# An expert layer's ranking: one head ranked while the scores are still copied, and the first round looked up in two pairs of heads

## The chip, the cores and the metric

The kernel runs on one core of a Trainium2 chip. The metric is the device time of one execution in microseconds (us). Three runs are shown for the kernel before; each kernel also has one execution recorded by the profiler, from which all durations here are taken. What matters of the core: TensorE multiplies (PE; PEld is its weight load), VectorE (DVE) and ScalarE (ACT) do the elementwise work, GpSimd (POOL) issues the indirect DMAs, and SyncE (SP) issues nearly all other loads, in the order in which they are written.

## The reference, cut to what matters

Two transformer blocks follow each other over 256 tokens of width 1024; the first is attention with a convolution, the second latent attention with gated linear attention. Each ends in the same kind of expert layer, with 8 heads, 128 keys per half and 16384 experts, of which each head of each token uses 16:

```
q = (h @ w_q).reshape(B, L, HEADS, 2, HALF)
s = einsum('blhpd,pnd->blhpn', q, sub_keys)               # 2 x 128 scores a head
top_s, top_i = top_k(s, 16)
cand_s = top_s[..., 0, :, None] + top_s[..., 1, None, :]  # 256 candidates
cand_i = top_i[..., 0, :, None] * NKEYS + top_i[..., 1, None, :]
best_s, best_pos = top_k(cand_s.reshape(..., 256), 16)
idx = take_along_axis(cand_i.reshape(..., 256), best_pos, axis=-1)
gate = softmax(best_s)
out = sum over heads and picks of (gate * gelu(u[idx] . h)) * v[idx]
```

## The kernel before, in words

**The expert layer is computed densely.** Instead of gathering rows, the kernel multiplies all 128 x 128 experts' `u` rows with all 256 tokens, applies gelu, multiplies each result by its gate (zero for an expert that a token did not pick), and multiplies with all `v` rows. Each of the two blocks (b = 1, 2) thus has these stages: `wq` (16 units of weights: the queries), scores, `u` (128 units), `v` (128 units). A unit is 512 KB, loaded by SP into a ring of four slots. Each unit is split into a high and a low part, in two halves of 128x512: ACT makes the high part (line 2320), DVE the low one (line 2323), and PE multiplies half by half (lines 935 to 937: three matmuls for each of a unit's eight 128-row parts, 24 a unit). The split parts have a ring of four halves (`HLRING`), so ACT and DVE can be at most four halves ahead of PE. ACT also applies gelu to each unit's result, two units behind (line 2358, `take_unit`).

**Scores and ranking.** PE computes the scores of two groups of 128 tokens, 16 score rows each (line 2276). ACT copies them to SBUF in eight pieces, each of two heads (`peer_act_scores`, line 2286). DVE waits for all eight (line 2793) and then ranks. The rank work of one head is nine slots (`topk_part`, lines 2368 to 2397: max, index and replace over both key halves, twice; 256 sums; the same over those). Four heads are a round; the four rounds are tokens 0 to 127 heads 0 to 3, heads 4 to 7, then the same for tokens 128 to 255. After the 36 slots of a round come 16 lookup slots (`lookup_part`, lines 2406 to 2449), which turn the picks into expert numbers and the best scores into gates: slot 0 converts and shifts the scores, slot 1 splits a position into its two ranks, slots 2 to 13 find the keys (12 operations of 512 elements: line 2424 compares, 2428 multiplies, 2430 sums), slots 14 and 15 normalise the gates and write the cells' numbers `picks_at`. A round has 52 slots (`ROUND_SLOTS`), all four 208.

**Where the slots go.** The u stage is written out for its first 111 units. DVE does one slot behind each half of a unit (`between(n)`, n the number of the half, line 2795), and a second one behind halves 7, 15, 23 and 31 (`LEAD`, `LEAD_EVERY`), so that it is four slots ahead from then on. The splits of halves 0 to 3 were made before the scores, so DVE starts with the slots and its first split is that of half 4. Between slot 14 and the gates, ACT's exp must have run: `peer_act` has it behind four fixed units (`exp_at`, line 2743). It changes ACT's function table, and the next gelu changes it back.

**The gates of tokens 0 to 127 go over DRAM.** Rounds 0 and 1 give 8 heads x 16 picks, which POOL scatters into `gates_dram[b]`, one indirect DMA of 128 cells for each of the 128 picks (`pool_scatter`, line 2477). Before the 16 DMAs of a head POOL waits until those of the head before have landed (they add to cells). Round i is released by `picks_ready` (line 2446). SP loads the gates back at the start of the v stage: `peer_loads` waits until all 128 scatters have landed (line 2903), loads the first four gate tiles (line 2885), and goes on with the v units (line 2911) and further gate tiles in turn. The four loads of v units 0 to 3 (line 2870) stand ahead of that wait. DVE multiplies activations by gates (line 2592), ACT and DVE split the product (lines 2648, 2654), and PE multiplies with v (lines 2243, 2244).

**The gates of tokens 128 to 255** are made by PE in the last 16 steps of the u stage from one-hot rows (line 2553); they need the end of round 3.

## Time and profile before

| | us |
|---|---|
| runs shown | 2224.8, 2226.89, 2227.07 |
| their median | 2226.89 |
| span of the profiled execution, first to last instruction | 2213.0 |
| time of the profiled execution around its span | not shown |
| PE busy | 2163.7 (98%) |
| DVE busy | 1691.2 (76%) |
| ACT busy | 1305.5 (59%) |
| POOL busy | 446.1 (20%) |
| mean granted clock of PE | 0.996 |

The span is the time from the first to the last instruction of one profiled execution; a run's time is that of the whole program. Busy shares are averages over stages. "Idle before" in a row is the time in which the row's engine did nothing ahead of it, and the arrow names what ended that time, as far as semaphores show it. The granted clock is the share of full speed that PE's clock had: 1.00 is 2.4 GHz and 0.50 is 1.2 GHz. All times of rows are us from the start of the span.

### The profile page before, as it was taken

What the parts mean: (1) busy time and instruction counts of PE and PEld (TensorE: products, weight loads), DVE (VectorE), ACT (ScalarE), POOL (GpSimd) and SP (SyncE); (2) the same over time, 40 slices, a digit from 0 to 9 for tenths busy, and PEclk for the clock granted to TensorE, in tenths of its full rate; (3) what the DMA queues carried; (4) which work ended last, traced back from release to release, by engine and by line L of the source; (5) the groups of instructions that cost most, each with busy time, mean ns of one, the idle gap of its engine ahead of it and who ended that gap; (6) DMA issues with size and microseconds to landing.
All of it is one profiled execution on the core that took longest, in us unless ns stands there. A gap on an engine that the chain in (4) does not pass through costs nothing.

```text
span 2213.0 us, 48254 instructions
## 1 busy us (share of the span) xinstructions
PE 2163.7 (98%) x15536; PEld 1992.3 (90%) x15536; DVE 1691.2 (76%) x3690; ACT 1305.5 (59%) x2727; POOL 446.1 (20%) x277
## 2 busy tenths in 40 slices
PE   8999999999999999999999999999999998999999
PEld 2888899999999888888889988999999997888887
DVE  4787769998889777777656866769988797777777
ACT  3577556556687555555555554656665695555554
POOL 0000000766674000000000000002666682000000
PEclk9999999999999999999999999999999999999999
DMA  8777545777755666666455434556777745666665
GB/s 329 262 238 246 176 148 188 200 194 191 198 136 134 217 214 213 212 214 214 151 162 176 149 108 151 198 162 191 198 192 195 190 112 149 214 213 214 213 213 169
DMA packets 191118, 422.88 MB, mean 191 GB/s; under 512 B 54288, under 2 KB 88336, under 8 KB 190624
## 3 DMA queue, kind: packets, MB, share of 16 engines
q1 hardware_dynamic: 150112, 413.73, 57.4%
q0 software_dynamic: 36864, 0.15, 4.5%
q10 hardware_dynamic: 4032, 7.64, 1.0%
q8 instruction: 56, 0.92, 0.2%
q14 instruction: 54, 0.44, 0.1%
HBM read 403.48 MB, written 17.96 MB: 190 GB/s over the span
## 4 chain that ended last, share of the span: by engine, by line
PE 92%; DVE 3%; ACT 2%; issue 1%; DMA 1%; POOL 0%; DVEq 0%; ACTq 0%; POOLq 0%
PE ps L2243 21%; PE ps L935 15%; PE ps L937 15%; PE ps L936 15%; PE ps L2244 11%; PE ps L960 5%; PE ps L2553 3%; PE ps L1866 1%; PE ps L1844 1%; DMA ring<-stream 1%; PE ps L2276 1%; PE ps L2166 1%; DVE ring_lo L614 1%; ACT arena L679 1%; PE ps L1858 1%
## 5 line engine op out<-in xcount | busy, mean ns | idle before, releaser
L2243 PE MATMUL ps<-csplit,hl 128*128 128x512 f32 x2048 | 711.9, 393 | 13.1 <-issue 12.0
L2477 POOL DMA_INDIRECT gates<-gbuf,picks_at x256 | 441.5, 1724 | 907.1 <-issue 482.9
L2244 PE MATMUL ps<-csplit,hl 128*128 128x256 f32 x2048 | 572.7, 280 | 0.0
L935 PE MATMUL ps<-hsplit,hl 128*128 128x256 f32 x2048 | 569.6, 278 | 0.0
L936 PE MATMUL ps<-hsplit,hl 128*128 128x256 f32 x2048 | 566.4, 277 | 0.0
L937 PE MATMUL ps<-hsplit,hl 128*128 128x256 f32 x2048 | 566.3, 277 | 0.0
L2320 ACT CAST hl<-ring 128x512 fp32r<-128x512 f32 x562 | 342.5, 620 | 263.7 <-PE ps L937 239.4
L2243 PEld LDWEIGHTS ps<-csplit,hl 128*128 128x128 f32 x2048 | 385.6, 188 | 98.9 <-issue 12.4
L2323 DVE TENSOR_TENSOR hl<-ring,hl 128x512 fp32r<-128x512 f32 x562 | 384.9, 690 | 87.7 <-ACT hl L2320 50.8
L2660 DVE TENSOR_TENSOR hl<-ring,hl 128x512 fp32r<-128x512 f32 x508 | 351.1, 692 | 68.7 <-ACT hl L2650 55.8
L2244 PEld LDWEIGHTS ps<-csplit,hl 128*128 128x128 f32 x2048 | 387.4, 189 | 0.0
L935 PEld LDWEIGHTS ps<-hsplit,hl 128*128 128x128 f32 x2048 | 384.9, 188 | 0.1
L936 PEld LDWEIGHTS ps<-hsplit,hl 128*128 128x128 f32 x2048 | 385.0, 188 | 0.0
L937 PEld LDWEIGHTS ps<-hsplit,hl 128*128 128x128 f32 x2048 | 384.5, 188 | 0.0
L2650 ACT CAST hl<-ring 128x512 fp32r<-128x512 f32 x508 | 314.4, 619 | 74.7 <-PE ps L2244 74.7
L2648 ACT CAST csplit<-arena 128x256 fp32r (+1 forms) x256 | 104.0, 406 | 243.9 <-DVE arena L2592 226.9
L2654 DVE TENSOR_TENSOR csplit<-arena,csplit 128x256 fp32r<-128x256 f32 x256 | 109.0, 426 | 123.0 <-ACT csplit L2648 123.0
L2358 ACT ACTIVATE arena<-ps 128x256 f32<-128x256 f32 (+1 forms) x272 | 103.1, 379 | 13.6 <-PE ps L937 12.2
L936 PE MATMUL ps<-n_hi,ring_lo 128*128 128x256 f32 (+1 forms) x352 | 99.7, 283 | 0.0
L2949 POOL MEMSET arena<- 128x1024 f32 x1 | 1.0, 951 | 422.9 <-PE ps L937 422.9
L2592 DVE TENSOR_TENSOR arena<-arena,gring 128x128 f32 (+1 forms) x256 | 72.6, 284 | 11.0 <-DMA gring<-gates 11.0
L686 DVE TENSOR_REDUCE arena<-arena 128x128 f32<-128x1024 f32 x32 | 62.3, 1950 | 17.6 <-ACT arena L679 17.6
(418 smaller groups left out, 3461.1 us busy)
## 6 DMA issues: line engine op xcount, KB each, us to landing
ring<-stream SPq DMA_DIRECT2D x675, 512.0 KB
s_area<-stream SPq DMA_DIRECT2D x48, 512.0 KB, 5.0
gates<-zeros SPq DMA_DIRECT2D x32, 512.0 KB, 5.1
gring<-gates SPq DMA_DIRECT2D x256, 64.0 KB, 4.1
gates<-gbuf,picks_at POOLq DMA_INDIRECT x256
arena<-xc ACTq DMA_DIRECT2D x2, 1024.0 KB, 15.5
arena<-keys ACTq DMA_DIRECT2D x2, 1024.0 KB, 6.7
gbuf<-consts ACTq DMA_DIRECT2D x1, 1120.0 KB, 5.1
```

The lines of the kernel that those rows point to most:

```text
L935: pe.matmul(out_ap, w[0], m[0], start=start, stop=False)
L936: pe.matmul(out_ap, w[1], m[0], start=False, stop=False)
L937: return pe.matmul(out_ap, w[0], m[1], start=False, stop=stop)
L960: mm = pe.matmul(ps[0:t.rows, t.bank, 0:t.cols], lhs, rhs, start=(t.start and i == 0), stop=(t.stop and i == last))
L2243: pe.matmul(ps[:, bank, :], w_hi, m_both, start=start, stop=False)
L2244: return pe.matmul(ps[:, bank, 0:T], w_lo, m_both[:, 0, :], start=False, stop=stop)
L2320: eng.copy(hl[:, hslot, 0, :], raw).then_inc(S("split_hi"), 1)
L2323: eng.tensor_tensor(hl[:, hslot, 1, :], raw, hl[:, hslot, 0, :].bitcast(F32), ALU.subtract)\
L2477: pool.indirect_dma_start(out=cells, out_offset=bass.IndirectOffsetOnAxis(ap=picks_at[:, i, c:c + 1], axis=0), in_=gates[:, i, c:c + 1], i ...
L2650: eng.copy(hl[:, hslot, 0, :], slot(unit)[:, part]).then_inc(S("split_hi"), 1)
L2654: ins = eng.tensor_tensor(csplit[:, cslot, 1, :], acts[:, c], csplit[:, cslot, 0, :].bitcast(F32), ALU.subtract)
L2660: eng.tensor_tensor(hl[:, hslot, 1, :], slot(unit)[:, part], hl[:, hslot, 0, :].bitcast(F32), ALU.subtract).then_inc(S("split_lo"), 1)
```

## The change

Three things are changed, all around the ranking, in both blocks.

- DVE waits for one of the eight score copies, not all, ranks the whole first head (nine slots), and only then waits for the other copies. From there `between(n)` does slot 9 + n behind each half n; the double slots are gone.
- Round 0 is cut in two pairs of heads. Each pair has 18 ranking slots and 8 lookup slots (`lookup_pair`): slot 0 does what slots 0 and 1 did, slots 1 to 6 are the 512-element operations, slot 7 does what slots 14 and 15 did. Each pair ends with its own `picks_ready`. Rounds 1 to 3 are as before.
- POOL waits for `picks_ready` before each head, for the first pair (heads 0, 1), the second (2, 3) or round 1. ACT's exp comes in five parts, the first two of 32 columns, behind units 6, 19, 41, 67 and 93.

```
-    LEAD, LEAD_EVERY = 4, 8
+    AHEAD = ITEM_SLOTS
+    PAIRS = 2
+    PAIR_SLOTS = ROUND_SLOTS // PAIRS
+    PARTS = PAIRS + ROUNDS - 1
...
+    def look_up(eng, x, c, step, out):
+        if step == 0:
+            rank = (rank1, rank2)[x][:, c].rearrange("p (r o) -> p r o", o=1).broadcast_to([P, 32, TOPK])
+            every = iota[:, 0:TOPK].rearrange("p (o a) -> p o a", o=1).broadcast_to([P, 32, TOPK])
+            eng.tensor_tensor(hit[:, c, :], rank, every, ALU.is_equal)
+        if step == 1:
+            keys = key_f[:, x, c].rearrange("p (h o a) -> p h o a", h=2, o=1).broadcast_to([P, 2, TOPK, TOPK])
+            h4 = hit[:, c, :].rearrange("p (h k) a -> p h k a", h=2)
+            eng.tensor_tensor(h4, h4, keys, ALU.mult)
+        if step == 2:
+            eng.tensor_reduce(out, hit[:, c, :], AX_X, ALU.add)
...
+    def lookup_pair(eng, b, pair, n):
+        c, heads = slice(pair * 32, pair * 32 + 32), slice(pair * 2, pair * 2 + 2)
+        best = picks_best[:, 0, :].rearrange("p (m k) -> p m k", k=TOPK)[:, heads, :]
+        g2 = gates[:, 0, :].rearrange("p (m k) -> p m k", k=TOPK)[:, heads, :]
+        if n == 0:
+            eng.tensor_copy(pos_f[:, c], picks_pos[:, c])
+            eng.tensor_copy(key_f[:, :, c], picks_key[:, :, c])
+            eng.tensor_tensor(g2, best, best[:, :, 0:1].broadcast_to([P, 2, TOPK]), ALU.subtract)\
+               .then_inc(S("gates_shifted"), 1)
+            eng.drain()
+            eng.tensor_scalar(rank1[:, c], pos_f[:, c], 1.0 / TOPK, -15.0 / 32, ALU.mult, ALU.add)
+            eng.drain()
+            eng.tensor_scalar(rank1[:, c], rank1[:, c], ROUND, ROUND, ALU.add, ALU.subtract)
+            eng.drain()
+            eng.scalar_tensor_tensor(rank2[:, c], rank1[:, c], -float(TOPK), pos_f[:, c], ALU.mult, ALU.add)
+        if 1 <= n < 7:
+            look_up(eng, (n - 1) // 3, c, (n - 1) % 3, chosen[:, (n - 1) // 3, c])
+        if n == 7:
+            eng.wait_ge(S("gates_exp"), PARTS * (b - 1) + pair + 1)
+            eng.tensor_reduce(gate_sum[:, 0, heads], g2, AX_X, ALU.add)
+            eng.scalar_tensor_tensor(chosen[:, 0, c], chosen[:, 1, c], float(P), chosen[:, 0, c], ALU.mult, ALU.add)
+            eng.drain()
+            eng.reciprocal(gate_sum[:, 1, heads], gate_sum[:, 0, heads])
+            eng.scalar_tensor_tensor(chosen[:, 0, c], chosen[:, 0, c], float(P), c_("token")[:, c], ALU.mult, ALU.add)
+            eng.drain()
+            z = gate_sum[:, 1, heads].rearrange("p (m o) -> p m o", o=1).broadcast_to([P, 2, TOPK])
+            eng.tensor_tensor(g2, g2, z, ALU.mult)
+            eng.tensor_copy(picks_at[:, 0, c], chosen[:, 0, c])
+            eng.drain().then_inc(S("picks_ready"), 1)
+        eng.drain()
...
+        ready = (PAIRS + 1) * (b - 1)
         for i in range(2):
-            pool.wait_ge(S("picks_ready"), 2 * (b - 1) + i + 1)
             for head in range(ITEMS):
+                pool.wait_ge(S("picks_ready"), ready + (1 + head // 2 if i == 0 else PAIRS + 1))
                 wait(pool, "scattered", 16 * sent)
...
-        exp_at = {(i * ROUND_SLOTS + ITEMS * ITEM_SLOTS - LEAD) // 2 + EXP_LAG: i for i in range(ROUNDS)}
+        shifted_at = [PAIR_SLOTS * pair + 2 * ITEM_SLOTS for pair in range(PAIRS)]
+        shifted_at += [ROUND_SLOTS * i + ITEMS * ITEM_SLOTS for i in range(1, ROUNDS)]
+        exp_at = {(n - AHEAD) // 2 + EXP_LAG: part for part, n in enumerate(shifted_at)}
...
-        dve.wait_ge(S("peer_s_copied"), 8 * b)
...
         def between(n):
-            done = n + min(n // LEAD_EVERY, LEAD)
-            ranking(done)
-            if n % LEAD_EVERY == LEAD_EVERY - 1 and n < LEAD * LEAD_EVERY:
-                ranking(done + 1)
+            ranking(AHEAD + n)
...
         def ranking(n):
             i, step = divmod(n, ROUND_SLOTS)
-            if i < ROUNDS and step < ITEMS * ITEM_SLOTS:
+            if i == 0:
+                pair, step = divmod(step, PAIR_SLOTS)
+                head, step = (2 * pair + step // ITEM_SLOTS, step % ITEM_SLOTS) if step < 2 * ITEM_SLOTS else (None, step)
+                if head is None:
+                    lookup_pair(dve, b, pair, step - 2 * ITEM_SLOTS)
+                else:
+                    topk_part(dve, 0, head, step)
+            elif i < ROUNDS and step < ITEMS * ITEM_SLOTS:
                 topk_part(dve, i, *divmod(step, ITEM_SLOTS))
...
+        dve.wait_ge(S("peer_s_copied"), 8 * (b - 1) + 1)
+        for n in range(AHEAD):
+            ranking(n)
+        dve.wait_ge(S("peer_s_copied"), 8 * b)
```

## Rows read from the trace of the kernel before

**Rows 1.** The page: span, and busy time of each engine (share of the span)

```profile
span 2213.0 us, 48254 instructions
...
PE 2163.7 (98%) x15536; PEld 1992.3 (90%) x15536; DVE 1691.2 (76%) x3690; ACT 1305.5 (59%) x2727; POOL 446.1 (20%) x277
```

**Rows 2.** Timeline, u to v in block 2: start, duration, engine, line, operation [idle before]

```profile
1842.11 0.28 PE L937 MATMUL ps<-hsplit,hl 128*128 128x256 f32 x1
...
1845.89 1.54 POOL L2477 DMA_INDIRECT gates<-gbuf,picks_at  x1 [1.90 <-issue]
...
1848.92 1.75 SPq L2885 DMA_DIRECT2D gring<-gates  x4
...
1852.19 0.76 PE L2243 MATMUL ps<-csplit,hl 128*128 128x512 f32 x1 [9.80 <-issue]
```

**Rows 3.** Waits of SP's queue: total us, times, longest

```profile
SPq L2885 <- DMA gates<-gbuf,picks_at: 9.0, 1, 9.0
```

**Rows 4.** Timeline, the same place in block 1

```profile
692.99 1.65 POOL L2477 DMA_INDIRECT gates<-gbuf,picks_at  x1 [0.30 <-issue]
...
700.91 1.86 SPq L2885 DMA_DIRECT2D gring<-gates  x4
...
703.10 0.28 PE L937 MATMUL ps<-hsplit,hl 128*128 128x256 f32 x1
...
705.63 0.76 PE L2243 MATMUL ps<-csplit,hl 128*128 128x512 f32 x1 [2.24 <-issue]
```

**Rows 5.** Timeline of POOL: the first scatter DMA of block 1 and of block 2

```profile
389.03 1.65 POOL L2477 DMA_INDIRECT gates<-gbuf,picks_at  x1 [387.58 <-DVEq L2446]
...
1528.38 1.56 POOL L2477 DMA_INDIRECT gates<-gbuf,picks_at  x1 [336.31 <-issue]
```

**Rows 6.** Timeline of ACT, block 1: the first of the eight score copies

```profile
317.84 0.69 ACT L2286 ACTIVATE s_area<-ps,small 128x512 f32<-128x512 f32 x1 [1.26 <-PE ps L2276]
```

**Rows 7.** Timeline of DVE, block 1: head 0, from its first slot to head 1

```profile
324.81 0.49 DVE L2370 MAX8 topbuf<-s_area 128x8 f32<-128x128 f32 x2 [7.51 <-ACT s_area L2286]
...
327.34 0.69 DVE L2323 TENSOR_TENSOR hl<-ring,hl 128x512 fp32r<-128x512 f32 x1
327.95 0.08 DVE L2382 MATCH_VALUE_LOAD picks_key<-topbuf,tmpbuf 128x8 f32 x1
...
333.47 0.69 DVE L2323 TENSOR_TENSOR hl<-ring,hl 128x512 fp32r<-128x512 f32 x1
```

**Rows 8.** PE in block 1: first u matmul (timeline), first gate matmuls (chain)

```profile
323.81 0.37 PE L935 MATMUL ps<-hsplit,hl 128*128 128x256 f32 x1
...
629.86 1.78 PE ps L2553 x16
```

**Rows 9.** Timeline of DVE, block 1: lookup slots of round 0 and splits

```profile
367.28 0.19 DVE L2407 CAST gbuf<-picks_pos 128x64 f32<-128x64 uint32 x1
...
369.27 0.69 DVE L2323 TENSOR_TENSOR hl<-ring,hl 128x512 fp32r<-128x512 f32 x1
...
370.64 0.69 DVE L2323 TENSOR_TENSOR hl<-ring,hl 128x512 fp32r<-128x512 f32 x1
...
386.28 0.21 DVE L2433 TENSOR_REDUCE gbuf<-gbuf 128x4 f32<-128x64 f32 x1
...
387.06 0.69 DVE L2323 TENSOR_TENSOR hl<-ring,hl 128x512 fp32r<-128x512 f32 x1
...
388.16 0.69 DVE L2323 TENSOR_TENSOR hl<-ring,hl 128x512 fp32r<-128x512 f32 x1 [0.17 <-issue]
```

**Rows 10.** Timeline of ACT, block 1: table load for the exp, and the one back

```profile
371.44 1.28 ACT L2749 ACT_TABLE_LOAD   x1
...
374.04 1.28 ACT L2358 ACT_TABLE_LOAD   x1
```

**Rows 11.** Stretches: us, busy (x) of PE, PEld, DVE, ACT, POOL, granted clock, DMA

```profile
705.60:708.70 3.10, 3.07 (x9) 2.67 (x10) 1.75 (x5) 0.80 (x3) 0.00 (x0) 0.50 0.34 100
...
1852.10:1855.50 3.40, 3.31 (x10) 2.86 (x11) 1.94 (x5) 1.37 (x4) 0.00 (x0) 0.50 0.60 187
```

More of the change, by code:

```diff
@@ L2420, in lookup_part @@
             c = slice(half * 32, half * 32 + 32)
-            if step == 0:
-                rank = (rank1, rank2)[x][:, c].rearrange("p (r o) -> p r o", o=1).broadcast_to([P, 32, TOPK])
-                every = iota[:, 0:TOPK].rearrange("p (o a) -> p o a", o=1).broadcast_to([P, 32, TOPK])
-                eng.tensor_tensor(hit[:, c, :], rank, every, ALU.is_equal)
-            if step == 1:
-                keys = key_f[:, x, c].rearrange("p (h o a) -> p h o a", h=2, o=1).broadcast_to([P, 2, TOPK, TOPK])
-                h4 = hit[:, c, :].rearrange("p (h k) a -> p h k a", h=2)
-                eng.tensor_tensor(h4, h4, keys, ALU.mult)
-            if step == 2:
-                eng.tensor_reduce(chosen[:, x, row][:, c], hit[:, c, :], AX_X, ALU.add)
+            look_up(eng, x, c, step, chosen[:, x, row][:, c])
         if n == 14:
-            eng.wait_ge(S("gates_exp"), ROUNDS * (b - 1) + i + 1)
+            eng.wait_ge(S("gates_exp"), PARTS * (b - 1) + PAIRS + i)
             eng.tensor_reduce(gate_sum[:, 0, :], g4, AX_X, ALU.add)
@@ L2746, in peer_act @@
             if s in exp_at:
-                i = exp_at[s]
-                act.wait_ge(S("gates_shifted"), ROUNDS * (b - 1) + i + 1)
-                act.activation(gates[:, i, :], gates[:, i, :], ACT.Exp).then_inc(S("gates_exp"), 1)
+                part = exp_at[s]
+                act.wait_ge(S("gates_shifted"), PARTS * (b - 1) + part + 1)
+                part_gates = gates[:, 0, part * 32:part * 32 + 32] if part < PAIRS else gates[:, part - PAIRS + 1, :]
+                act.activation(part_gates, part_gates, ACT.Exp).then_inc(S("gates_exp"), 1)
         first = groups_of(0)
```

## The prediction, made before the changed kernel was run

> **What bounds the kernel now.** I read the page's totals first: TensorE (PE) is busy for 98% of the 2213.0 us span [rows 1], so only a stretch in which PE stands still can be worth anything. The longest waits of PE put one such stretch at the start of the second block's v stage: PE ends its last u matmul at 1842.39 (1842.11 + 0.28) and starts its first v matmul at 1852.19, after 9.80 us idle [rows 2]. The "issue" behind that number names nothing, so I went to SP's own list of waits: SP stands 9.0 us at L2885, the load of the first gates, for the scatter's DMAs [rows 3]. In time the chain is: POOL issues the last scatter DMA at 1845.89, SP issues the gate loads at 1848.92, PE starts 3.27 us later [rows 2]. Hence **the scatter is late by 9.0 us in block 2, and PE pays for it**.
>
> Block 1 shows the same place without that wait. The last scatter DMA is issued at 692.99, about 8 us before SP comes to the gate loads at 700.91; PE is idle from 703.38 to 705.63, which is 2.24 us [rows 4]. This is the floor of the hand-over, set by SP's order (the gates go out behind the four v loads) and the path over DVE and ACT. In both blocks SP comes to the gate loads 2.47 us before the last u matmul ends (703.38 - 700.91; 1842.39 - (1848.92 - 9.0) = 2.47). So block 2 without the scatter's wait should look like block 1.
>
> **When the scatter runs.** In block 1 its 128 DMAs are issued from 389.03 to 694.64, 306 us or 2.39 us for each; in block 2 they start at 1528.38 and end at 1847.43 (1845.89 + 1.54), 319 us or 2.49 us for each [rows 2, 4, 5]. POOL has nothing before it; it waits for DVE's ranking.
>
> **The change, part by part.**
>
> *Scores copied while head 0 is ranked.* ACT makes eight copies of 0.69 us, the first from 317.84 to 318.53 [rows 6]; DVE has nothing to do for 7.51 us and starts ranking at 324.81 [rows 7]. The nine steps of head 0 cost, from 324.81 to 333.47 without the four splits between them (0.61 us each from 327.34 to 327.95), 8.66 - 2.44 = 6.22 us [rows 7]. Started at 318.53 they end at 324.75, just as the last copy ends. Cover: the copies. If it is gone, up to 6.22 us fall on DVE (rival 3). The head reads only the first copied bank, and a wait for one copy suffices.
>
> *Ranking ahead by nine slots, no double slots.* Before, DVE did 36 steps in the first 32 halves and was four ahead from then on; now it is nine ahead from the start and does one a half. DVE's work from half 4 to 32 thus falls by four steps, about 4 x 0.69 us. That matters, because DVE had no slack here: PE starts half h at about 323.81 + 1.36 h (323.81 for half 0, and 629.86 for the gate matmuls behind half 223, 224 halves later) [rows 8]; DVE begins split 47 at 387.06 and ends it at 387.75 [rows 9], and half 47 is due at 387.7 to 388.0. The old order was tight to a few tenths of a us.
>
> *Lookup in two pairs.* What a round of four heads did in 16 slots is now 2 x 8 slots. Six of each eight are the same 512-element instructions as before, 1.37 us with the split (369.27 to 370.64) [rows 9]. The other two hold what filled four slots. The first: full width it costs 369.27 - 367.28 - 0.61 = 1.38 us; the last: 388.16 - 386.28 - 0.61 = 1.27 us [rows 9]. A pair has half the columns, so each lies between one half (0.69 and 0.64) and the whole; for small instructions I take the whole, the nearest row. Then, by hand: split 9 starts at 334.1, split 10 at 334.1 + 0.61 + 1.38 = 336.1, split 16 six slots later at 344.3, the pair is ready at 344.3 + 0.61 + 1.27 = 346.2, and split 17 ends at 346.9. Half 17 is due at 323.81 + 17 x 1.36 = 346.9. So PE waits for 0 to 0.3 us there, and as much at half 43 with the second pair; I take 0 and keep 4 x 0.3 = 1.2 us for the range.
>
> A rule that speaks against this part: the Trainium skill ("VectorE: DVE Perf Modes", section on the TRN2 errata) says that an operation from SBUF pays a fixed cost per instruction beside its columns, so halving the width does not halve the time. By its formula, 32 fewer columns at 0.96 GHz save an estimated 0.03 us of each of 14 instructions, 0.2 us in a slot; the sum is the same with it, since split 17 is then in time by some tenths. With the halved prices it would be in time by over 1 us. No row here shows both widths of one instruction.
>
> *One more exp on ACT.* It costs ACT a table load of 1.28 us before it and one behind it; from the first to the second it also did the exp and the next two copies, 374.04 - 371.44 = 2.60 us [rows 10]. The new ones stand behind units 6 and 19. PE ends half 9 near 323.81 + 13.6 = 337.4; behind it ACT does copy 13 and a take (I take 1.1 us), and then these 2.60 us: copies 14 and 15 are there at 341.1, and DVE wants copy 14 at 344.3 - 2 x 1.37 = 341.6. Cost 0; it waits for `gates_shifted`, which DVE gives at half 9, before ACT gets there; queued behind it are ACT's copies for halves 14 and 15.
>
> *The scatter starts earlier.* Before, the first DMA came 0.87 us behind the end of DVE's last slot (388.16 to 389.03) [rows 5, 9]. Now it comes at 346.2 + 0.9 = 347.1, or 42 us earlier; in block 2 at about 1486.4. Its new waits: heads 2 and 3 need the second pair, ready at half 42 (about 382), and POOL gets to them after 32 DMAs, 347.1 + 32 x 2.49 = 427. Round 1 is ready five halves earlier than before, near 451, and POOL gets there at 347.1 + 64 x 2.49 = 506. Neither wait is felt. SP has nothing new in its order. In block 2 the scatter ends at 1486.4 + 319 = 1805, and SP comes to the gates at 1839.9. **It is early by 34 us**, so even 10% more per DMA costs nothing. In block 1 nothing is gained, since it was early already.
>
> *What is late next.* The path of block 1: from the gates' issue to the first v matmul 4.72 us (700.91 to 705.63) against 3.27 us in block 2 [rows 2, 4]. With 4.72 the start is 1839.92 + 4.72 = 1844.64 instead of 1852.19: 7.55 us gained. With 3.27 it is 9.0 us. I take 7.55, since then the loads meet the v loads, as in block 1. The clock: after either gap (2.24 and 9.80 us) the granted clock is 0.50, the 1.2 GHz level, for a little over 3 us [rows 11]; so that loss stays, and a gap as short as block 1's does not spare it.
>
> **Sum.** -7.55 (block 2's hand-over) + 0 (everything else) on a profiled span of 2213.0 us. The median of the shown runs is 2226.89, 13.9 us above the span; I take this as what lies around it, the same before and after. 2226.9 - 7.5 = 2219.4 us. A measurement here tells about 0.2%, 4.5 us, from no change.
>
> **Rivals.**
> 1. *The wait is not there in ordinary runs, or the scatter ends no earlier* (18%). The 9.0 us are one execution; a scatter 3% quicker than the profiled one has no wait to lose, and a POOL held up by something else (a full queue: it has pauses of 2 to 5 us now) would end as late as before. Against: 319 us of scatter with a 34 us margin, and 306 us in block 1. Time: 2226.9, or 2223 with half the wait.
> 2. *More than the floor* (7%). The gates land in 3.27 us, so PE is idle for 0.8 us only, and the clock stays high: 9.0 + about 1.5 us (five pairs of matmuls in 3.1 us that would take half as long). Time 2226.9 - 10.5 = 2216.4. Against: the clock row of block 1.
> 3. *The nine steps are not under the copies* (5%). Place: the start of each u stage. If DVE gets going only behind the last copy, or slows the copies, it is 6.22 us late with 1.26 us of slack at half 4 (due 329.3, split ends at 328.03): PE stands 5.0 us a block, and the restart at the low clock costs 1.5 more: 2 x 6.5 - 7.5 = +5.5, 2232.4 us. It decides once head 0 ends over 5 us behind the last copy (7.5 / 2 + 1.26). For it: DVE was without slack up to half 47. Against: the first bank is copied 6.3 us before the last.
>
> **The numbers.** The forecast has 70%, its own range being 2217.5 to 2221.5. The range must leave no more than 2 in 10 out: it reaches down to rival 2 and up to rival 1, 2216.5 to 2227.2. Faster by over 0.2%: the forecast, rival 2 and a small part of rival 1, 0.76; the same 0.19; slower 0.05.
>
> **What would show it.** POOL's first scatter DMA near 347 and 1486; its last in block 2 near 1804, before SP's gate loads; SP's wait at L2885 gone; PE's gap at the v stage of block 2 at 2.2 us instead of 9.8; the first MAX8 at 318.5, and PE without idle time around halves 17 and 43. Wrong if PE shows gaps in the u stage, if the first v matmul of block 2 still waits for the scatter, or if the gap shrinks in the profile and the runs do not follow.

## The result, and the profile after

| | before | after |
|---|---|---|
| median of the runs, us | 2225.24 (2219.74 to 2227.07, 5 runs) | 2211.13 (2208.31 to 2221.41, 5 runs) |
| ratio, 95% interval | | 0.9943 [0.9916, 0.9970] |
| span of the profiled execution, us | 2213.0 | 2219.6 |

The kernel became faster, by 14 us in the medians against 7.5 foretold, and 2211.13 lies below the range (2216.5 to 2227.2). Meanwhile the profiled execution of after is *longer* than that of before, by 6.6 us. Both need explaining, and the pace of PE, found below, has a part in both. The 14 us are also partly the luck of five runs each: over all groups below the mean gain is 9.1 us.

Here are the page's totals of after, then the timeline at the end of block 2's u stage (start, duration, engine, line, operation, [idle before]), which answers to [rows 2]:

```profile
span 2219.6 us, 48312 instructions
PE 2176.5 (98%) x15536; PEld 2003.8 (90%) x15536; DVE 1695.6 (76%) x3714; ACT 1310.8 (59%) x2733; POOL 433.1 (20%) x277
```

```profile
1796.20 1.54 POOL L2517 DMA_INDIRECT gates<-gbuf,picks_at  x1 [4.21 <-issue]
...
1855.69 1.86 SPq L2935 DMA_DIRECT2D gring<-gates  x4
...
1857.88 0.28 PE L937 MATMUL ps<-hsplit,hl 128*128 128x256 f32 x1
...
1860.45 0.47 PE L2243 MATMUL ps<-csplit,hl 128*128 128x512 f32 x1 [2.29 <-issue]
```

**The hand-over is as foretold.** The last scatter DMA goes out 59 us before SP comes to the gates, SP's list of waits no longer has the scatter in it, and PE is idle for 2.29 us instead of 9.80. From the first gate matmul to the first v matmul of block 2 it is 75.92 us instead of 83.43: 7.51 us gained, against 7.55 foretold. The starts of the scatter also come where they were put (POOL's timeline, block 1 and block 2):

```profile
350.36 1.65 POOL L2517 DMA_INDIRECT gates<-gbuf,picks_at  x1 [348.92 <-DVEq L2487]
...
1490.75 1.56 POOL L2517 DMA_INDIRECT gates<-gbuf,picks_at  x1 [294.46 <-issue]
```

Here the u stage began 3.61 us later (327.42 against 323.81), so 350.36 is 346.75 on before's time axis; 347.1 was forecast.

**The early head fits under the copies.** Timeline of block 1, head 0 and the first and last score copy:

```profile
321.45 0.69 ACT L2289 ACTIVATE s_area<-ps,small 128x512 f32<-128x512 f32 x1 [1.26 <-PE ps L2279]
322.17 0.49 DVE L2373 MAX8 topbuf<-s_area 128x8 f32<-128x128 f32 x2 [1.25 <-ACT s_area L2289]
...
327.71 0.69 ACT L2289 ACTIVATE s_area<-ps,small 128x512 f32<-128x512 f32 x1 [0.21 <-PE ps L2279]
...
328.43 0.49 DVE L2373 MAX8 topbuf<-s_area 128x8 f32<-128x128 f32 x2
```

Head 0 takes 322.17 to 328.43, 6.26 us (6.22 foretold), and head 1 starts just as the last copy ends.

**The pair's two crowded slots.** DVE's timeline, block 1: first and last instruction of slot 0, then of slot 7, each with the split behind it:

```profile
338.30 0.17 DVE L2464 CAST gbuf<-picks_pos 128x32 f32<-128x32 uint32 x1
...
339.28 0.19 DVE L2473 SCALAR_TENSOR_TENSOR gbuf<-gbuf 128x32 f32<-128x32 f32 x1
339.55 0.69 DVE L2326 TENSOR_TENSOR hl<-ring,hl 128x512 fp32r<-128x512 f32 x1
...
348.37 0.18 DVE L2478 TENSOR_REDUCE gbuf<-gbuf 128x2 f32<-128x32 f32 x1
...
349.16 0.17 DVE L2486 CAST picks_at<-gbuf 128x32 uint32<-128x32 f32 x1
349.50 0.69 DVE L2326 TENSOR_TENSOR hl<-ring,hl 128x512 fp32r<-128x512 f32 x1 [0.17 <-issue]
```

They cost 339.55 - 338.30 = 1.25 us and 349.50 - 348.37 = 1.13 us, where 1.38 and 1.27 were taken at full width: half the columns saved 0.13 and 0.14. The Trainium skill ("VectorE: DVE Perf Modes", section on the TRN2 errata) has a fixed cost per instruction, and this trace agrees: the same CAST takes 0.17 us at 32 columns and 0.19 at 64 [rows 9]. Split 17 starts at 349.50 and ends at 350.2; PE comes to that half at 327.42 + 17 x 1.36 = 350.5. So it is in time with 0.3 us to spare, and PE has no gap in either u stage of this execution.

**Where the 6.6 us went.** I cut both executions at PE's starts (us): scores to first gate matmul (u), first gate matmul to first v matmul (hand-over), and what lies between.

| profiled execution | time | start to scores | u, block 1 | hand-over 1 | v 1 to scores 2 | u, block 2 | hand-over 2 | rest |
|---|---|---|---|---|---|---|---|---|
| before | | 316.64 | 313.22 | 75.77 | 750.56 | 312.57 | 83.43 | 360.81 |
| after | 2221.41 | 320.26 | 313.04 | 75.69 | 751.84 | 323.70 | 75.92 | 359.15 |

Block 2's u stage is **11.1 us longer** in after, without a gap. The stretches of 50 us show how (us, busy and matmuls of PE, PEld, DVE, ACT and POOL, granted clock, DMA share, GB/s), after and then before:

```profile
400.00:450.00 50.00, 50.00 (x443) 50.00 (x443) 45.35 (x119) 30.43 (x58) 35.14 (x22) 1.00 0.76 197
550.00:600.00 50.00, 50.00 (x444) 50.00 (x443) 43.53 (x108) 30.31 (x59) 33.94 (x20) 1.00 0.77 191
1550.00:1600.00 50.00, 50.00 (x427) 50.00 (x427) 43.84 (x115) 29.61 (x57) 36.99 (x23) 1.00 0.74 187
1700.00:1750.00 50.00, 50.00 (x427) 50.00 (x426) 41.92 (x105) 29.78 (x57) 36.85 (x22) 1.00 0.76 188
```

```profile
400.00:450.00 50.00, 50.00 (x444) 50.00 (x443) 45.47 (x127) 30.56 (x59) 36.78 (x23) 1.00 0.79 191
...
1600.00:1650.00 50.00, 50.00 (x443) 50.00 (x443) 44.75 (x138) 28.17 (x56) 32.51 (x21) 1.00 0.77 194
```

PE is busy throughout, the granted clock is 1.00, and yet it does 427 matmuls in 50 us in one stage and 443 in the other: 1.41 us a half of a unit, or 1.36. I call these **the 1.41 pace and the 1.36 pace**. That makes the profiled executions of before and after incomparable in length, although each of their hand-overs can be compared.

### The profile page after: what moved, and what is told of

Its sections match the earlier page's. It is cut to its first block, busy times and chain, and to the rows that moved or that the text cites. A ratio compares the mean times of both kernels' runs of the same rounds, so it can differ in the third digit from the quotient of the medians.

```text
span 2219.6 us, 48312 instructions
## 1 busy us (share of the span) xinstructions
PE 2176.5 (98%) x15536; PEld 2003.8 (90%) x15536; DVE 1695.6 (76%) x3714; ACT 1310.8 (59%) x2733; POOL 433.1 (20%) x277
## 4 chain that ended last, share of the span: by engine, by line
PE 91%; DVE 3%; ACT 2%; DMA 1%; issue 1%; POOL 0%; DVEq 0%; SPq 0%; ACTq 0%; POOLq 0%
PE ps L2243 21%; PE ps L935 15%; PE ps L937 15%; PE ps L936 15%; PE ps L2244 11%; PE ps L960 5%; PE ps L2593 3%; DMA ring<-stream 1%; PE ps L1866 1%; PE ps L1844 1%; PE ps L2279 1%; PE ps L2166 1%; DVE ring_lo L614 1%; ACT arena L679 1%; PE ps L1858 1%
## 5 line engine op out<-in xcount | busy, mean ns | idle before, releaser
L2517 POOL DMA_INDIRECT gates<-gbuf,picks_at x256 | 428.5, 1674 | 832.6 <-issue 447.3
L2361 ACT ACTIVATE arena<-ps 128x256 f32<-128x256 f32 (+1 forms) x272 | 103.1, 379 | 13.4 <-PE ps L937 12.1
```

The lines of the kernel that those rows point to most:

```text
L2517: pool.indirect_dma_start(out=cells, out_offset=bass.IndirectOffsetOnAxis(ap=picks_at[:, i, c:c + 1], axis=0), in_=gates[:, i, c:c + 1], i ...
```

## The experiments

Each kernel is one edit of before or of after. Ratios are to before, run on the same chip in the same group; its median there stands with the first run of each group.

### The two kernels again, and the two halves of the change

First group; before 2225.27 (35 runs). `before_again` and `after_again` are unedited. `front_only` is before with the early head and without the double slots, its round 0 in one piece:

```
-    LEAD, LEAD_EVERY = 4, 8
+    AHEAD = ITEM_SLOTS
...
-            done = n + min(n // LEAD_EVERY, LEAD)
-            ranking(done)
-            if n % LEAD_EVERY == LEAD_EVERY - 1 and n < LEAD * LEAD_EVERY:
-                ranking(done + 1)
+            ranking(AHEAD + n)
...
+        dve.wait_ge(S("peer_s_copied"), 8 * (b - 1) + 1)
+        for n in range(AHEAD):
+            ranking(n)
```

`pairs_only` is after with no early head and with the double slots of before back in place.

> The kernel before, unchanged, as a control, with a new profile. Three theories for a gain of 12.7 us where 7.55 was forecast. T1: the change is worth the hand-over of block 2 alone (7.5 us); the rest is the pace of PE in a u stage, which has two levels in the two profiles (444 and 427 matmuls in 50 us, 11 us over a stage) and falls by chance. T2: in ordinary executions the scatter of the kernel before ends later than in its profile, and the wait at the gates is 12 to 20 us. T3: the order of DVE's and ACT's slots at the start of the u stage sets PE's pace, so that the change itself moves it. Time: T1, T2 and T3 all 2225 us, ratio 1.000. Profile: T1 a hand-over of block 2 of 8 to 11 us, and either pace; T2 a hand-over of 12 to 20 us at the fast pace; T3 a hand-over near 10 us and the slow pace in at least one u stage.

> The changed kernel, unchanged, as a control, with a new profile. Hand-over of block 2 near 1.6 us under all three. T1: ratio 0.9966 on enough runs, any pace. T2: ratio 0.992 to 0.994. T3: ratio 0.992 to 0.994, and the fast pace in both u stages more often than in the kernel before.

> Only the first part: head 0 ranked during the copies, nine slots ahead, no double slots; round 0 is looked up whole. The scatter starts near 382 instead of 389, and ends some 7 us earlier than before. T1: the wait of block 2 shrinks from 9.0 to about 2 us, the hand-over to about 3 us, gain about 7 us, ratio 0.997. T2: gain 7 us only, with 5 to 12 us of wait left, ratio 0.997. T3: the whole gain of 12.7 us or near it, ratio 0.9943, because the double slots are gone.

> Only the second part: round 0 in two pairs, scatter started by the first pair (near 356, 33 us earlier than before), with the wait for all eight copies and the double slots as before. DVE has no slack here: the first slot of a pair's lookup is 1.3 us, on top of double slots, so PE may stand for up to 1 us around halves 21 and 47 in each block. T1: gain 7.5 us less up to 2, ratio 0.997. T2: the whole gain, 0.994. T3: no gain from the pace, as the double slots stay: 0.997.

| | median (range, runs) | ratio, 95% interval |
|---|---|---|
| before_again | 2228.20 (2218.73 to 2232.62, 12) | 1.0021 [0.9996, 1.0046] |
| after_again | 2209.65 (2206.38 to 2220.03, 12) | 0.9936 [0.9916, 0.9957] |
| front_only | 2212.52 (2203.66 to 2230.04, 12) | 0.9947 [0.9921, 0.9973] |
| pairs_only | 2229.51 (2219.87 to 2239.20, 12) | 1.0023 [1.0001, 1.0046] |

Before's second profile has the 1.41 pace in both blocks (us, PE busy, granted clock, DMA share, GB/s), and its list of SP's waits has no scatter wait:

```profile
400.00:450.00 50.00, 50.00 (x427) 1.00 0.73 184
...
1550.00:1600.00 50.00, 50.00 (x427) 1.00 0.74 188
```

A u stage at the 1.41 pace gives the scatter 11 us more, so the 9.0 us wait of [rows 3] is not there. **Pairs alone**, which release the scatter in time for block 2 just as the whole change does, are 20 us slower than the changed kernel. Their PE stands at halves 17 and 24, where the double slots now meet the crowded slots of a pair, for 0.2 to 0.8 us each, and both u stages go over to the 1.41 pace: block 1 at half 17, block 2 at half 22, two halves ahead of the longer of its stops. A reading formed: the stops are small, but PE's pace after them costs up to 11 us a block.

**The first part alone has the whole gain.** front_only, whose round 0 is not cut in pairs, comes out at a ratio of 0.9947, where T3 had 0.9943 and T1 and T2 had 0.997 (0.9973 is the end of the interval, so they are not quite excluded). Its mean lies 10.4 us under before (4.9 to 15.5) and 3.4 us over after_again, with an interval from 1.7 us under to 8.8 us over. Its scatter starts only some 7 us earlier in the u stage than before's. So the part of the change that was made for the scatter, the pairs, wins nothing measurable on top of the part that gives DVE more room.

### Stalls placed by hand

Second group; before 2226.72 (31 runs). All three are after with four more operations of 0.69 us on DVE in each block, at different halves:

```
+            for _ in range({20: 4}.get(n, 0)):
+                dve.tensor_tensor(hit[:, 0:32, :], hit[:, 0:32, :], hit[:, 0:32, :], ALU.max)
+                dve.drain()
```

`stall_late` has `{180: 4}`, `work_spread` one each behind halves 64, 72, 124 and 180. `lead0` is before with `LEAD, LEAD_EVERY = 0, 8`: no double slots, so its scatter starts later and DVE has less to do early.

> The changed kernel with four more DVE operations (128x512, 0.76 us each with their drain) behind half 20 of both u stages, where DVE has about 0.9 us of slack: PE stands for about 2.1 us there. The first runs showed that PE holds one pace per burst, 1.36 or 1.41 us a half, and that a kernel with short stalls (pairs only) went from the first to the second behind its stall. T3, now: every stall, however short, draws the pace of the rest of the stage anew, mostly the slow one. Then each block loses 2.1 us and 0.053 us for each of 201 halves, 12.8 us: 25 us over the changed kernel, 2235 us, and the profile shows 1.36 before and 1.41 behind the stall. T1, where the pace falls by chance at the start of a stage alone: only the stalls, 4 us, 2214 us, and one pace on both sides of the stall.

> The same four operations behind half 180 in both blocks, where DVE has about 1.5 us of slack: PE stands for about 1.5 us. T3: the slow pace holds for the 41 halves left only, 2 x (1.5 + 2.2) = 7 us, 2217 us. T1: 3 us, 2213 us. The difference to the stall behind half 20 is 18 us under T3 and 1 us under T1.

> The same four operations, one each behind halves 64, 72, 124 and 180, where the slack of 1.5 to 2.2 us covers one: no stall. T3 and T1: the time of the changed kernel, 2210 us, ratio to the kernel before 0.993. If more DVE work alone costs time, it is over 2213 us.

> The kernel before without its four double slots (LEAD 0, not 4): DVE's slack at halves 16 to 47 rises from 0.0-0.4 to over 1 us, and the scatter is released four halves, 5.5 us, later. Where PE is fast in block 2, the wait at the gates must grow from 9.0 to about 14.5 us; where it is slow, the stage is 11 us longer and the wait about 3 us. T3: the stalls of the tight halves are gone, so the fast pace holds more often, and the two effects nearly meet: 2220 us, that is below the kernel before (2225) although its scatter is later. T1: the same mix of paces as before and a later scatter, 2228 us.

| | median (range, runs) | ratio, 95% interval |
|---|---|---|
| stall_early | 2223.64 (2218.52 to 2231.14, 10) | 0.9998 [0.9974, 1.0021] |
| stall_late | 2220.67 (2212.63 to 2234.74, 10) | 0.9999 [0.9970, 1.0028] |
| work_spread | 2214.39 (2207.77 to 2222.16, 10) | 0.9956 [0.9930, 0.9981] |
| lead0 | 2228.63 (2220.62 to 2233.25, 10) | 1.0015 [0.9990, 1.0039] |

The work as such is nearly free: work_spread has a ratio of 0.9956, near that of the changed kernel, though its 2214.39 is over the 2213 us set for it (this group has no run of after). The same work as one stall is not free: 9 us between the medians of work_spread and stall_early. But the 2235 us expected of stall_early was a miss, and so was its profile. PE stands for 2.1 us in each block and then goes on at the **1.36** pace (PE's timeline, then stretches as above, the last one right behind the stall):

```profile
357.81 0.36 PE L935 MATMUL ps<-hsplit,hl 128*128 128x256 f32 x1 [2.08 <-DVE hl L2326]
...
1501.82 0.36 PE L935 MATMUL ps<-hsplit,hl 128*128 128x256 f32 x1 [2.10 <-DVE hl L2326]
```

```profile
400.00:450.00 50.00, 50.00 (x444) 1.00 0.75 193
1550.00:1600.00 50.00, 50.00 (x444) 1.00 0.73 193
...
1501.80:1506.00 4.20, 4.18 (x22) 0.59 0.73 151
```

The stalls need no change of pace to cost 9 us: in this profile the halves up to 212 take 3.95 us more in block 1 and 4.25 us more in block 2 than the same halves of a stage of after at 1.36. Of that some 2.2 us are the standing, and most of the rest is the low granted clock behind it, 0.59 in the stretch shown, with matmuls every 0.213 us for a time.

"A stall costs the pace" is thus refuted as a rule; stall_late's block 1 did fall to the 1.41 pace behind its short stalls at halves 181 to 183, and its median of 2220.67 is above both forecasts (2217 and 2213). lead0 was a miss for T3 too, which had 2220; its 2228.63 is what T1 gave. SP waits for the scatter in both blocks, in block 2 for 9.1 us where 14.5 were expected, and nothing is seen to be won by the lighter start.

```profile
SPq L2885 <- DMA gates<-gbuf,picks_at: 14.8, 2, 9.1
```

### Without the scatter

Third group; before 2229.58 (29 runs). Both kernels leave out the scatter, and with it the gates of tokens 0 to 127; POOL only waits for the picks:

```
-        for i in range(2):
-            for head in range(ITEMS):
...
+        pool.wait_ge(S("picks_ready"), 2 * b)
```

> The kernel before without the scatter DMAs (the gates of tokens 0 to 127 are left out); SP waits for the zeroed gates instead, which are there long before. No wait at the gates is left in any execution, and DVE's and ACT's order is that of the kernel before, with 0.15 us of slack at half 32. Fast executions 2208 us. Theory A (the wait alone: the ordinary wait of the kernel before is larger or more frequent than in its profile, and the order on DVE does nothing): as fast as the kernel after, ratio to before 0.994. Theory B (the order on DVE: the tight halves let PE stand for a moment now and then, and the rest of the stage runs at the slow pace): only the wait's share is gained, ratio 0.997 to 0.999, and times over 2218 us stay frequent.

> The changed kernel without the scatter DMAs. Its scatter is early anyway, so both theories: the time of the changed kernel, 2209 us, ratio 0.993 to 0.994. Against the kernel before without its scatter: A the same time within 2 us, B 5 to 8 us less. If the scatter's DMAs themselves push PE to the slow pace, it is 3 us or more below the changed kernel.

> The changed kernel once more, on the chip of the two runs without a scatter: ratio to the kernel before 0.9936 if the earlier value holds on another chip; 0.9966 if chance gave the rest. Both u stages at 1.36 us a half in more than half of the executions (times under 2213 us).

| | median (range, runs) | ratio, 95% interval |
|---|---|---|
| before_no_scatter | 2226.30 (2203.24 to 2234.55 and one of 9258.12, 12) | 0.9977 [0.9954, 1.0001] |
| after_no_scatter | 2219.97 (2206.01 to 2234.50, 12) | 0.9958 [0.9931, 0.9986] |
| after_third (after, unedited) | 2219.45 (2207.95 to 2233.00, 12) | 0.9961 [0.9939, 0.9983] |

The ratio leaves the run of 9258.12 out. With no scatter to wait for, before gains 3 us in the medians and 6.2 us (0.8 to 12.5) in the means of its other eleven runs. The two orders of DVE's work differ by 6 us in the medians and 3 us in the means, with an interval from 10.5 us one way to 5.0 us the other: a lead, no proof. By the ratios before_no_scatter came where theory B had it (0.997 to 0.999) and not at A's 0.994; after_no_scatter missed its 0.993 to 0.994, and after_third was near the 0.9966 set for chance. And after itself is 2219.45 here, 10 us above its first groups, with before 4 us up: how often the 1.41 pace comes differs from group to group.

### Short stalls, and more spare time

Fourth group; before 2222.64 (35 runs). `after_fourth` is after, `pairs_again` is pairs_only, `stall_short` is stall_early with `{20: 2}`. `slack` is after with ten lookup slots for a pair, not eight, so that each crowded slot is two again:

```
-    PAIR_SLOTS = ROUND_SLOTS // PAIRS
+    PAIR_SLOTS = 2 * ITEM_SLOTS + 10
+    FIRST_SLOTS = PAIRS * PAIR_SLOTS
...
-            eng.drain()
+        if n == 1:
             eng.tensor_scalar(rank1[:, c], pos_f[:, c], 1.0 / TOPK, -15.0 / 32, ALU.mult, ALU.add)
...
-            eng.drain()
+        if n == 9:
             z = gate_sum[:, 1, heads].rearrange("p (m o) -> p m o", o=1).broadcast_to([P, 2, TOPK])
```

> The changed kernel, unchanged, as the control of this group. All theories: ratio 0.992 to 0.997 against the kernel before (2208 to 2220 us).

> The pairs without the early head, as before. Its scatter is released in time, so by the gates alone it should win the same 7.5 us as the changed kernel (ratio 0.9966). Theory P (PE's stalls of 0.3 to 0.9 us near halves 17 and 25 put the rest of the stage at the slow pace of 1.41 us a half, up to 11 us a block): 0.998 to 1.006, and in the profile at least one of the two u stages falls from 444 to about 427 matmuls in 50 us right behind such a stall.

> The changed kernel with two 128x512 operations more of DVE behind half 20 of each block, 1.4 us of work against about 0.6 us of slack. Rival P2 (only a stall under 1 us costs the pace): PE stands for 0.3 to 1 us near half 22 and goes on at the slow pace, 1.41 us a half for the 200 halves left, +10 us in each block that was fast: 9 to 20 us over after_fourth. Rival N (the pace is drawn anew at every restart, short or long, mostly fast): +1.4 us for the stalls and a few us for the draws: 2 to 6 us over after_fourth. Rival Z (the length of a stall says nothing and pairs_only was slow by chance): +1.4 us.

> The changed kernel with ten lookup slots for a pair, not eight: the first of the eight is two again, and so is the last, so that no slot of a pair has more than about 0.7 us of small instructions. The ranking ends four halves later, round 1 is ready 5.4 us later. If the halves with under 0.5 us to spare cost the changed kernel pace: 1 to 5 us under after_fourth. If they cost nothing, the same within 2 us. A scatter that started 1.4 us later in each block costs nothing in either case.

A fifth group (before 2229.38, 20 runs) repeated the last of them with its control.

> The same as slack, for its difference from the changed kernel, which the first group left at -3.0 us with an interval of -8.4 to +2.8 us. If more spare time on DVE keeps the fast pace: 2 to 8 us under after_fifth again. If the first group was chance: within 2 us of it.

> The changed kernel as the control of slack_again: 0.992 to 0.998 of the kernel before.

| | median (range, runs) | ratio, 95% interval |
|---|---|---|
| after_fourth | 2218.46 (2207.30 to 2228.63, 12) | 0.9970 [0.9944, 0.9995] |
| pairs_again | 2230.49 (2220.47 to 2233.19, 12) | 1.0030 [1.0007, 1.0052] |
| stall_short | 2223.93 (2210.29 to 2235.51, 12) | 1.0007 [0.9981, 1.0034] |
| slack | 2212.18 (2207.02 to 2231.96, 12) | 0.9954 [0.9931, 0.9977] |
| slack_again | 2209.84 (2207.07 to 2232.09, 9) | 0.9938 [0.9907, 0.9969] |
| after_fifth | 2220.67 (2207.73 to 2235.45, 12) | 0.9979 [0.9950, 1.0008] |

pairs_again came where theory P had it (0.998 to 1.006), stall_short near rival N's 2 to 6 us over its control, and after_fourth and after_fifth inside what was set for them. pairs_again also shows a change of pace at a single late split. PE's timeline in block 1 (start, duration): the matmuls follow each other every 0.113 us, one comes 0.34 us after the last, since DVE's split ended only at 353.65, and from there on they follow every 0.118 us:

```profile
353.35 0.28 PE L936 MATMUL ps<-hsplit,hl 128*128 128x256 f32 x1
353.47 0.28 PE L937 MATMUL ps<-hsplit,hl 128*128 128x256 f32 x1
353.81 0.36 PE L935 MATMUL ps<-hsplit,hl 128*128 128x256 f32 x1
354.00 0.28 PE L936 MATMUL ps<-hsplit,hl 128*128 128x256 f32 x1
354.12 0.28 PE L937 MATMUL ps<-hsplit,hl 128*128 128x256 f32 x1
354.24 0.28 PE L935 MATMUL ps<-hsplit,hl 128*128 128x256 f32 x1
354.35 0.28 PE L936 MATMUL ps<-hsplit,hl 128*128 128x256 f32 x1
```

The stretches behind it in block 1, and in block 2, where the gaps at halves 17 and 24 (0.32 and 0.96 us from start to start) changed nothing, the pace went over to 1.41 at half 45 without a gap, and the gap of 0.32 us at half 48 brought 1.36 back:

```profile
364.40:414.40 50.00, 50.00 (x425) 1.00 0.73 185
1550.00:1600.00 50.00, 50.00 (x444) 1.00 0.75 198
```

In stall_short the gaps of block 1 (0.80 and 0.39) left the pace at 1.36, the one of block 2 (1.05) brought 1.41:

```profile
400.00:450.00 50.00, 50.00 (x443) 1.00 0.77 197
1550.00:1600.00 50.00, 50.00 (x427) 1.00 0.74 180
```

So the length of a stall does not decide. **Nor is a gap needed.** Where PE waited for a split, its first matmul began 0.14 to 0.16 us behind the split's end (here 353.65 to 353.81); a half that starts so had nothing to spare. Such a start leaves a mark: the first matmul takes 0.34 to 0.36 us instead of 0.28, and the next follows 0.18 to 0.20 us behind it. The mark also stands where PE lost next to nothing. The changed kernel has one at half 17, behind the last crowded slot of its first pair, in block 2 of stall_early, stall_late, stall_short and work_spread, all four unedited up to there. In stall_late the split ends at 1488.47, the matmul comes on the beat, and yet the pace changes (DVE's timeline, PE's timeline, PE's stretches on either side):

```profile
1487.78 0.69 DVE L2326 TENSOR_TENSOR hl<-ring,hl 128x512 fp32r<-128x512 f32 x1 [0.16 <-issue]
```

```profile
1488.52 0.28 PE L937 MATMUL ps<-hsplit,hl 128*128 128x256 f32 x1
1488.63 0.34 PE L935 MATMUL ps<-hsplit,hl 128*128 128x256 f32 x1
1488.81 0.28 PE L936 MATMUL ps<-hsplit,hl 128*128 128x256 f32 x1
```

```profile
1475.00:1488.00 13.00, 13.00 (x117) 1.00 0.57 193
1490.00:1503.00 13.00, 13.00 (x113) 1.00 0.78 207
```

**The kernel before has the mark too**, at half 32 in both blocks of its profile and of before_no_scatter's, that is in all four of its u stages that ran at 1.36. Its timelines of DVE and PE, block 1, where the step is 0.195 us instead of 0.113 (the pace stayed at 1.36 in these four):

```profile
366.67 0.69 DVE L2323 TENSOR_TENSOR hl<-ring,hl 128x512 fp32r<-128x512 f32 x1
```

```profile
367.32 0.28 PE L937 MATMUL ps<-hsplit,hl 128*128 128x256 f32 x1
367.51 0.36 PE L935 MATMUL ps<-hsplit,hl 128*128 128x256 f32 x1
```

The five profiles of after, lead0 and front_only have no such mark (front_only's two stages ran at 1.41 from their start). The count over the 19 profiles, up to half 212: of 24 marks met at the 1.36 pace, the pace went over to 1.41 at nine; of eight met at 1.41, it came back to 1.36 at five. Twice more it went to 1.41 without a mark, at splits that ended 0.22 us ahead of PE. At the start of a u stage, behind the scores, 10 of the 38 stages took the 1.41 pace. **So a restart of PE, or a split that comes just in time, can change the pace, either way; counted together the 1.41 pace comes in about three of ten.**

It is not a coin with fixed odds, though. Near half 212 every u stage has a gap of 0.36 us, in which PE does three small matmuls for something else. Behind it the pace is 1.36 in block 2 of all 19 profiles and 1.41 in block 1 of 16 of them (all but pairs_only, pairs_again and slack), whatever it was ahead of it. Before's profile, on either side of it in block 1 and then in block 2:

```profile
598.00:610.00 12.00, 12.00 (x108) 1.00 0.85 208
616.00:628.00 12.00, 12.00 (x104) 1.00 0.77 198
1738.00:1750.00 12.00, 12.00 (x108) 1.00 0.89 209
1756.00:1768.00 12.00, 12.00 (x108) 1.00 0.72 200
```

What the pace depends on at such a place no run here shows.

What makes this dear is that it is lopsided: at 1.36 a tight half stops PE and the pace falls anew; once at 1.41 every later split has more time (0.05 us more with each half), so fewer are tight. An estimate, as if each restart were a draw of three in ten: a stage that meets no gap is slow in 0.3 of the cases; one with two gaps early on in 1 - 0.7 x 0.7 x 0.7 = 0.66. Two stages, (0.66 - 0.30) x 10 us each, give 7 us, and the standing itself about 1 us: 8 us for the pairs alone over the changed kernel. The means of the runs differ by 18 us in the first group and by 12.1 (7.7 to 16.5) in the fourth: right in kind, too small in size. One gap, as in stall_short, gives (0.51 - 0.30) x 10 x 2 = 4 us and 1 to 2 of standing; measured 6.5 (0.8 to 12.0).

**More spare time seems to help.** slack lies under its control in both groups, by 3.0 and 7.1 us in the means. Neither difference is clear by itself (-8.4 to +2.8 and -14.0 to +0.3); together they are -5.0 us with an interval of -9.5 to -0.4 (the runs of each kernel drawn again 20000 times). The profiles of after have no mark that it could remove, but the four at half 17 above are at the slot that slack divides, and two of these four stages went over to 1.41 there. That it works this way is argued, not shown: slack's own two profiles took the 1.41 pace at the start of the stage, the first in both blocks, the second in block 2. Its means, 2213.9 and 2213.8, are the lowest of these two groups; after_again, in the first group, had 2210.8.

**What the runs of before say.** An execution of before with both stages at 1.36 takes 2214.8 us by its profile (its span and the 1.8 us that the other runs have around theirs). An estimate from that, with 11.1 us for a stage at 1.41 and the wait gone when it is block 2's: 2218 with block 2 at 1.41, 2226 with block 1, 2229.5 with both (before_again: 2228.93). If the 1.41 pace came in three of ten stages, some seven in ten of the runs would be near 2215 or 2218. Of the 124 runs of before measured beside a run of after only 26 are at 2220 or less. For the 53 runs of after the share fits: 23 are at 2212 or less, and half were to be expected (after_again and after_fifth, both stages at 1.36: 2209.76 and 2211.08). So before takes the 1.41 pace in most of its ordinary executions, and after in about three of ten stages. That before's tight halves (32 without any spare time, 24 and 43 to 47 with 0.1 us) are the reason fits all of this, but no profile here caught before changing its pace at one.

## Why the prediction was wrong, point by point

- **The hand-over, -7.55 us: right between the two profiles.** 7.51, by the mechanism named: the scatter ends before SP comes, and the floor of block 1 is reached. For the ordinary run it was taken at full price, see below. Its start, its end (1797.7; 1805 was forecast, and the stage began 4.6 us later, so it ran 12 us quicker than the 319 us taken) and the gap of 2.29 us all came as said.
- **The early head at no cost: right** (6.26 us under the copies). Rival 3 did not come.
- **The pair's crowded slots: right in price, a little dear** (1.25 and 1.13 us against 1.38 and 1.27). No gap at halves 17 and 43 in after's profiles; but with after's order PE met half 17 with nothing to spare in 4 of the 17 u stages that were at 1.36 there.
- **"So that loss stays" of the clock: partly wrong.** The stretch behind block 1's gap has a granted clock of 0.50, as before; block 2's has 1.00, at nearly the same idle time (2.16 and 2.29 us):

```profile
709.00:712.20 3.20, 3.20 (x10) 2.72 (x11) 1.73 (x4) 0.95 (x3) 0.00 (x0) 0.50 0.41 128
1860.40:1862.00 1.60, 1.55 (x9) 1.42 (x10) 1.60 (x5) 0.73 (x2) 0.00 (x0) 1.00 0.48 174
```

  Rival 2 had this as a part of its gain, 1.5 us; in the table it sits in the rest, 359.15 against 360.81. It is not the change's: other profiles of after have 360.7 there.
- **"I take this as what lies around it, the same before and after", 13.9 us: wrong, and the step that failed.** In the runs with both numbers an execution's time is its span + 1.8 us (2221.41 and 2219.6). So before's profiled execution took about 2214.8 us, and only 10 of the 124 runs of before are as short as that. It had the 1.36 pace in both blocks, and the 9.0 us wait in full; the median run, by its time, has at least one stage at 1.41. Of the 13.9 us only 1.8 lie around the span. The rest was a property of that execution, and I carried it as a constant.
- **"PE waits for 0 to 0.3 us there ... I take 0 and keep 4 x 0.3 = 1.2 us for the range": wrong as a price.** A late split, or one just in time, costs itself and can change the pace, worth up to 11 us for the rest of the stage. I had written that the old order "was tight to a few tenths of a us" and gave its relief no price at all. front_only, pairs_only and stall_short show that such spare time is worth microseconds, in both directions. Half 32 of before, whose rows are above, was already without any, and I had looked at half 47 only.
- **Rival 1, "the wait is not there in ordinary runs": right about the wait, wrong about the time.** The wait is not there in an execution whose block 2 runs at the 1.41 pace, as before_again shows. It also needs a scatter of over 310 us (319 - 9.0) in block 2, as the rival said. The 319 us are the longest of the 17 profiles that have a scatter; the others have 299 to 315, before_again 309.5, and only lead0 is above 310. And the six shortest of the 124 runs of before, 2208.8 to 2212.8, are 2 to 6 us shorter than its profiled execution, in which both stages were already at 1.36. The time did not stay near 2226.9, since the change won by the pace what it did not win at the wait.
- **The range** had no term for the pace at all. Of five measurements of the same changed kernel the medians are 2211.13, 2209.65, 2219.45, 2218.46 and 2220.67: three lie inside 2216.5 to 2227.2. The mean gain over the five is 9.1 us, with an interval of 7.1 to 11.1 (53 runs of after, 124 of before). The forecast of -7.5 lies in it, but that is luck in good part: most of these 9.1 us are not the hand-over's. The level it was set on, and its width, failed too.

**What stays open.** How the 9.1 us divide is not measured. The hand-over gives 7.5 us only where block 2 of before is at 1.36 and its scatter is slow. An estimate from the means: before's 2225.3 lies 10.5 us above its profiled execution, which is 0.7 of its stages at 1.41 (11.1 us for block 1, 11.1 - 7.5 = 3.6 for block 2); after's 2216.6 lies 6.2 us above the 2210.4 of after_again's and after_fifth's profiled runs, which is 0.3. Then the hand-over gives at most 0.3 x 7.5 = 2 us and the pace the rest. Also open are what sets the pace at a restart, why its share differs between groups, and why lead0, which has no mark, gained nothing.

## What to carry to other kernels

Before using a profiled execution as a base, set its time (span and the little around it) against the runs: if it lies at their edge, cost the edit for an ordinary execution also, and ask which waits vanish there. Where PE is the bound and is fed just in time, look for the half with the least spare time, and price the spare time of its feeders, not only their lateness: a stall of 0.3 us, or a split just in time, can cost 10 us, while four operations placed where there is room cost next to nothing. Judge such an edit by many runs of both kernels on one chip; five runs could not tell 7 us from 14.

## What the hardware showed that I had not expected

- **TensorE keeps one of two paces for hundreds of microseconds, at a granted clock of 1.00**: a 128x256 matmul every 0.113 us or every 0.118 us (443 or 427 in 50 us), 3.7% apart. In 38 u stages no steady stretch was in between. The pace can change at a gap of 0.34 us or with no gap at all (stall_late, half 17), and can stay through one of 0.96 us. The Trainium skill ("TensorE: Matmul & The Clock Gate", section on the back-to-back issue gap) gives columns over 2.4 GHz and 2.5 ns for a matmul by itself at full clock, 109 ns as an estimate for 256 columns, and says that a stream with a weight load for each matmul differs from it. It has no value for such a stream at 256 columns. The 1.36 pace is 4 ns above that estimate and the 1.41 pace 9. The granted clock does not explain the two, since it is the same in both.
- The v stages show no such choice: 291 matmuls in 50 us at 750 to 800 us in each of the five executions looked at, those with either pace in their u stages among them.
- The granted clock was 0.50 behind a gap of 2.16 us in one block of an execution (after) and 1.00 behind one of 2.29 us in the other.
